# Expert token rows taken from a scattered DRAM buffer and eight transposes instead of sixteen 0/1 matmuls per turn

## The reference

```python
top_logit, top_e = lax.top_k(logits, TOP_K)              # 2 of 8 experts for each token
gate = jax.nn.softmax(top_logit, axis=-1)
...
xb = xt[buf_tok].reshape(n_blk, MOE_BLOCK, d)            # blocks of 128 token rows of one expert
def expert_block(args):
    xblk, e = args
    g, u = jnp.split(xblk @ w_in[e], 2, axis=-1)
    return (jax.nn.silu(g) * u) @ w_out[e]
yb = lax.map(expert_block, (xb, blk_e)).reshape(cap, d)
out = jnp.zeros((n_tok, d), h.dtype).at[buf_tok].add(yb * buf_w[:, None])
```

## Time and profile before

| | us |
|---|---|
| median of 3 runs | 1537.06 (1536.93 to 1539.17) |
| the profiled execution | 1536.48 |
| its span | 1534.8 |
| busy: PE | 1492.7 (97%) |
| busy: DVE | 1202.3 (78%) |
| busy: ACT | 967.4 (63%) |
| busy: POOL | 62.1 (4%) |
| DMA | 425.79 MB, mean 277 GB/s |

### The profile page before, as it was taken

How to read it: one execution, slowest core, us unless ns; L and a number is a source line. 1 busy time by engine, 2 the same in 40 slices (tenths; PEclk the granted TensorE clock), 3 DMA queues, 4 the chain that set the end, 5 groups by cost and what they waited for, 6 DMA issues and landing times.

```text
span 1534.8 us, 20546 instructions
## 1 busy us (share of the span) xinstructions
PE 1492.7 (97%) x7544; PEld 1230.2 (80%) x7544; DVE 1202.3 (78%) x1073; ACT 967.4 (63%) x895; POOL 62.1 (4%) x90
## 2 busy tenths in 40 slices
PE   8999999999999899999999999999999999999995
PEld 6867889998767588888888888888888888888884
DVE  5757464554656799898899888989989989988988
ACT  4645444443344477777677777777777777777774
POOL 1023200000021100000000000000000000000000
PEclk9999999999989999999999999999999999999998
DMA  9741255556503599999999999999999999999990
GB/s 328 176 140 56 70 178 178 180 192 185 172 18 139 207 350 350 341 377 348 362 352 344 377 350 354 343 363 366 342 350 371 345 342 380 344 376 347 335 344 27
DMA packets 200922, 425.79 MB, mean 277 GB/s; under 512 B 10384, under 2 KB 42160, under 8 KB 200880
## 3 DMA queue, kind: packets, MB, share of 16 engines
q1 hardware_dynamic: 196864, 419.65, 76.3%
q10 hardware_dynamic: 4016, 5.56, 1.1%
HBM read 424.14 MB, written 1.05 MB: 277 GB/s over the span
## 4 chain that ended last, share of the span: by engine, by line
PE 90%; DVE 4%; ACT 4%; issue 1%; DMA 1%; ACTq 0%; DVEq 0%
PE bank L922 26%; PE bank L924 26%; PE bank L923 26%; PE bank L1137 2%; PE bank L939 2%; PE bank L1309 2%; ACT wh L863 2%; PE bank L1168 2%; PE bank L1371 2%; DVE wl L1858 1%; PE bank L951 1%; DVE wl L1402 1%; ACT L863 1%; PE bank L1324 0%; PE bank L1325 0%
## 5 line engine op out<-in xcount | busy, mean ns | idle before, releaser
L922 PE MATMUL bank<-wh,arena_r 128*128 128x512 f32 x1432 | 564.4, 394 | 2.6 <-DVE wl L1858 1.4
L1858 DVE TENSOR_TENSOR wl<-ring,wh 128x2048 fp32r<-128x2048 f32 x224 | 511.3, 2291 | 66.3 <-ACT wh L863 65.7
L924 PE MATMUL bank<-wl,arena_r 128*128 128x512 f32 x1432 | 558.1, 390 | 0.0
L923 PE MATMUL bank<-wh,arena_r 128*128 128x512 f32 x1432 | 557.5, 389 | 0.0
L863 ACT ACTIVATE wh<-ring 128x2048 fp32r<-128x2048 f32 x224 | 428.9, 1917 | 92.5 <-PE bank L924 92.4
L922 PEld LDWEIGHTS bank<-wh,arena_r 128*128 128x128 f32 x1432 | 268.9, 188 | 61.5 <-DVE wl L1858 6.4
L924 PEld LDWEIGHTS bank<-wl,arena_r 128*128 128x128 f32 x1432 | 268.8, 188 | 57.0
L923 PEld LDWEIGHTS bank<-wh,arena_r 128*128 128x128 f32 x1432 | 269.1, 188 | 53.7
L1402 DVE TENSOR_TENSOR wl<-ring,wh 128x2048 fp32r<-128x2048 f32 (+1 forms) x64 | 144.5, 2263 | 94.1 <-ACT wh L651 94.0
L651 ACT ACTIVATE wh<-ring 128x2048 fp32r<-128x2048 f32 (+1 forms) x64 | 120.8, 1893 | 114.6 <-PE bank L924 110.0
L1858 DVE TENSOR_TENSOR wl<-arena,wh 128x2048 fp32r<-128x2048 f32 x64 | 146.6, 2291 | 20.2 <-ACT wh L863 20.2
(11 more groups left out here) (246 smaller groups left out, 1363.5 us busy)
## 6 DMA issues: line engine op xcount, KB each, us to landing
ring<-in_moe_w_in_dram SPq DMA_DIRECT2D x171, 1024.0 KB
ring<-in_moe_w_out_dram SPq DMA_DIRECT2D x56, 1024.0 KB
arena<-in_moe_w_out_dram SPq DMA_DIRECT2D x40, 1024.0 KB, 6.0
slot<-in_moe_w_in_dram SPq DMA_DIRECT2D x32, 1024.0 KB, 5.2
arena<-in_moe_w_in_dram SPq DMA_DIRECT2D x24, 1024.0 KB, 6.3
ring<-in_dense_w_in_dram SPq DMA_DIRECT2D x22, 1024.0 KB
slot<-in_moe_w_out_dram SPq DMA_DIRECT2D x16, 1024.0 KB, 5.9
ring<-in_dense_w_out_dram SPq DMA_DIRECT2D x11, 1024.0 KB
```

The lines of the kernel that those rows point to most:

```text
L922: pe.matmul(out_, lh, rh, start=start, stop=False, skip_group_check=True)
L923: pe.matmul(out_, ll, rh, start=False, stop=False, skip_group_check=True)
L924: return pe.matmul(out_, lh, rl, start=False, stop=stop, skip_group_check=True)
L1858: dve.tensor_tensor(wl[:, n % SPLITS, :], slot_at[SLOT[k % PER_EXPERT]], wh[:, n % SPLITS, :].bitcast(F32), ALU.subtract).then_inc(split, 1)
```

## The change

1. A DRAM buffer `xb` of 17 blocks of 128 rows by 1024 float32 (8.9 MB) is filled with zeros: POOL clears 512 columns of the arena (`zeros`) after the first layer norm, and ACT issues two DMAs at c = 3 of the dense mixer, each of 128x17 pieces of 2 KB.
2. DVE works out, ahead of the loop of turns, the row of `xb` for each of the two experts of each token (eight small instructions behind `take_rows(1)`); POOL then issues four indirect DMAs, each of which scatters 128 rows of 4 KB of `h` into `xb`.
3. SP loads 128 rows (512 KB) for the next turn into `xg`, which is `h[:, 0, :]`, ahead of item 16 of each turn. In turn 0 it waits there for the four scatters, for `pre`, and for the first gather.
4. In the loop PE does eight transposes of `xg` (`turn_rows`) instead of `gather`, after a wait for that load. The gather ahead of the loop stays. `build_pick` leaves the loop on DVE.

The diff, cut to its core:

```diff
+ROWS_AT = 16
...
+        zeros = room(12288, 512)
+        xg = h[:, 0, :]
...
+        xb = nc.dram_tensor("xb", [(2 * NE + 1) * P, D], F32)
+        xb_by_turn = xb.rearrange("(s p) n -> s p n", p=P)
...
             for k in range(PER_EXPERT):
+                if k == ROWS_AT:
+                    sp.wait_ge(scattered, 16 * 4)
+                    sp.wait_ge(e_added, 1)
+                    sp.wait_ge(e_rows, 2)
+                    sp.dma_start(xg, xb_by_turn[1]).then_inc(xg_landed, 16)
                 expert_item(0, k, 0, first=True)
...
                 for k in range(PER_EXPERT):
+                    if k == ROWS_AT:
+                        sp.wait_ge(e_rows, 2 * i + 2)
+                        sp.dma_start(xg, xb_by_turn[ds(i + 1, 1)].rearrange("e p n -> (e p) n")).then_inc(xg_landed, 16)
                     expert_item(i, k, i % NE)
...
+            pool.wait_ge(h_ready, 4)
+            pool.memset(zeros, 0.0).then_inc(zeros_ready, 1)
             pool.wait_ge(h_ready, 8)
...
             pool.tensor_scalar(pre[:, :, :], h[:, :, :], ALPHA, None, ALU.mult).then_inc(e_added, 1)
+            pool.wait_ge(zero_filled, 16 * 2)
+            pool.wait_ge(rows_ready, 1)
+            for tt in range(NT):
+                for k in range(2):
+                    pool.indirect_dma_start(xb[:, :], bass.IndirectOffsetOnAxis(ap=rows_i[:, k, tt, :], axis=0),
+                                            h[:, tt, :], None).then_inc(scattered, 16)
...
                     act_e.activation(silu[:, c % 2, :], bank[2 * (c % 2)][:, :], ACT.Silu).then_inc(silu_ready, 1)
+                    if c == 3:
+                        act_e.wait_ge(zeros_ready, 1)
+                        for half in range(2):
+                            act_e.dma_start(xb_by_turn[:, :, 512 * half:512 * half + 512].rearrange("s p n -> p s n"),
+                                            zeros.rearrange("p (s n) -> p s n", s=1).to_broadcast([P, 2 * NE + 1, 512]))\
+                                 .then_inc(zero_filled, 16)
...
+            def turn_rows(i):
+
+                pe.wait_ge(xg_landed, 16 * i + 16)
+                for c in range(DC):
+                    ins = pe.transpose(bank[2 + c // 4][:, (c % 4) * P:(c % 4) * P + P], xg[:, c * P:c * P + P], ident[:, :])
                     if c % 4 == 3:
                         ins.then_inc(e_rows, 1)
...
-                            gather(i + 2)
+                            turn_rows(i)
...
             take_rows(1)
+
+            step(dve.tensor_scalar(best, at_rank, float(P), float(NE * P - P), ALU.is_gt, ALU.mult))
+            step(dve.tensor_tensor(best, best, at_rank, ALU.add))
+            step(dve.tensor_tensor(best, best, first_row[:, :, :], ALU.add))
+            for k, chosen in enumerate((pick1, pick2)):
+                step(dve.tensor_tensor(rest, best, chosen, ALU.mult))
+                step(dve.tensor_reduce(rows_f[:, k, :, :], rest, X, ALU.add))
+            dve.tensor_copy(rows_i[:, :, :, :], rows_f[:, :, :, :]).then_inc(rows_ready, 1)
...
                         elif what == "build":
-                            build_pick(ds(i + 1, 1), i + 1)
                             dve.wait_ge(e_putT, i + 1)
```

More of the change, by code:

```diff
@@ L199, in decoder_kernel @@
         std = sb("std", [P, NT, 2])
-        lg = sb("lg", [P, 7, NT, NE])
+        lg = sb("lg", [P, 8, NT, NE])
         selb = sb("selb", [P, NT, NE], BF16)
@@ L206, in decoder_kernel @@
         turns_i = sb("turns_i", [P, 1], I32)
+        first_row = sb("first_row", [P, NT, NE])
+        rows_f = sb("rows_f", [P, 2, NT, 1])
+        rows_i = sb("rows_i", [P, 2, NT, 1], I32)
         base = [-(-nc.sbuf_base // 64) * 64]
@@ L362, in decoder_kernel @@
         done = sem("done")
+        zeros_ready = sem("zeros_ready")
+        zero_filled = sem("zero_filled")
+        rows_ready = sem("rows_ready")
+        scattered = sem("scattered")
+        xg_landed = sem("xg_landed")
+        xb = nc.dram_tensor("xb", [(2 * NE + 1) * P, D], F32)
+        xb_by_turn = xb.rearrange("(s p) n -> s p n", p=P)
         in_a = w_in_a[0].rearrange("(c p) n -> p c n", p=P)
@@ L581, in _ @@
                            allow_small_or_imprecise_dtypes=True))
+            step(pool.iota(first_row[:, :, :], [[0, NT], [P, NE]], base=-1, channel_multiplier=0,
+                           allow_small_or_imprecise_dtypes=True))
             step(pool.memset(cmp_in[:, :, :, :], 0.0))
@@ L1301, in _, with gather @@
               .then_inc(ranked, 1)
-            def gather(value):
-                pe.wait_ge(e_pick, value)
+            def gather():
+                pe.wait_ge(e_pick, 1)
                 for c in range(DC):
@@ L1310, in gather @@
                                         pick[:, tt, :], start=(tt == 0), stop=(tt == NT - 1))
+                    if c % 4 == 3:
+                        ins.then_inc(e_rows, 1)
+            def turn_rows(i):
+                pe.wait_ge(xg_landed, 16 * i + 16)
+                for c in range(DC):
+                    ins = pe.transpose(bank[2 + c // 4][:, (c % 4) * P:(c % 4) * P + P], xg[:, c * P:c * P + P], ident[:, :])
                     if c % 4 == 3:
@@ L1330, in _ @@
             keep_warm(2, 4)
-            gather(1)
+            gather()
             pe.wait_ge(plan_ready, 1)
@@ L1741, in _, with build_pick @@
             split_weights(N_FIRST + SPLITS)
-            def build_pick(at, value):
-                if value is not None:
-                    dve.wait_ge(e_rows, 2 * value)
+            def build_pick():
                 for tt in range(NT):
-                    ins = dve.tensor_scalar(pick[:, tt, :], slots[:, :], slotx[:, tt, at], None, ALU.is_equal)
+                    ins = dve.tensor_scalar(pick[:, tt, :], slots[:, :], slotx[:, tt, 0:1], None, ALU.is_equal)
                 ins.then_inc(e_pick, 1)
             logits = bank[6][:, 256:256 + NT * NE].rearrange("p (t e) -> p t e", t=NT)
-            best, pick1, rest, pick2, sel, gw, tmp = (lg[:, k, :, :] for k in range(7))
+            best, pick1, rest, pick2, sel, gw, tmp, at_rank = (lg[:, k, :, :] for k in range(8))
             wide = [P, NT, NE]
@@ L1775, in _ @@
             step(dve.tensor_scalar(tmp, bank[7][:, 0:NT * NE].rearrange("p (t e) -> p t e", t=NT), 1.0, None, ALU.add))
[L1776 to L1779, removed]
+            step(dve.tensor_tensor(at_rank, tmp, sel, ALU.mult))
+            step(dve.tensor_scalar(slotx[:, :, 0:NE], at_rank, -1.0, None, ALU.add))
+            build_pick()
+            step(dve.tensor_scalar(slotx[:, :, NE:2 * NE], at_rank, -1.0 - P, None, ALU.add))
             step(dve.tensor_reduce(cnt[:, 0:1], bank[7][:, 2 * NE:3 * NE], X, ALU.max))
```

## The result

The changed kernel takes **1517.45 us** (1515.84 to 1517.85, 4 runs). The kernel before, run beside it, took 1538.12 us (1536.93 to 1539.36, 4 runs). The ratio is 0.9864, 95% interval 0.9846 to 0.9881: 20.7 us faster. The profiled execution took 1517.43 us, its span is 1515.7.

A forecast was written before the change was run, and what follows sets the result against it. PE was taken to bound the kernel, a turn lasting 123.88 us. Only the gather counted: 8 x 2.62 = 21.0 us off 1536.48 gives 1515.5, plus 0.6 for the median, 1516 us; all else nothing; range 1513 to 1528.

The forecast's parts named there:

- Part 1, the gather: End of each turn on PE: 3.50 us of gather become 0.88 of transposes, 2.62 less, 21.0 us in eight turns.
- overshoot: Gain beyond the idle time of ACT and DVE behind the gather, 0.4 to 0.5 us a turn; at most 3.8 us.
- Part 2, the fill: Zero fill issued by ACT in the dense mixer: costs nothing, hidden by ACT's idle time and three split items.
- the low side: Lower bound on ACT's standing at the fill: two issues of 0.45 us, 0.9 us; the upper bound was 16.1.
- The free time: How long ACT may stand at the fill's issues in the dense mixer before PE waits: 9.7 us.
- Part 3, numbers and scatter: Turn 0: eight small instructions in DVE's 4.65 us pause, scatter landing between 533.6 and 555; costs nothing.
- The deadline: Latest end of the scatter in turn 0 that still lets SP load item 16 in time: 558 us.
- Part 4, the row load: SP's extra load in each turn: traffic rises from 355.5 to 367 GB/s, with room; costs nothing.
- DMA as the bound: Rival, in the turns: mixed stream holds only 358 GB/s, a turn takes 124.5 us, 1542 in all; chance 0.09.
- ACT held: Rival, at the fill: ACT's issues hold it until PE stands 6.4 us and the clock falls; 1524; chance 0.14.
- scatter late: Rival, turn 0: at 10 us per indirect DMA the scatter ends 14 us late; 1530; chance 0.06, late fill included.
- Part given back: Rival, at each turn's end: 3.8 us of the gain is lost again, 1520; chance 0.10.

The follow-up runs named there:

- the rest alone: Changed kernel with the gather and its comparisons back in the loop; fill, row numbers, scatter and row loads stay, rows loaded but unused: 1537.31 us, ratio 1.0002.
- the third transfer's run: Changed kernel with one more fill transfer of 4.5 MB, into a second buffer, behind the two on ACT: 1525.99 us, ratio 0.9928.
- sixteen scatters: Changed kernel with twelve more indirect DMAs into other buffers ahead of the four, SP waiting for all: 1521.21 us, ratio 0.9902.
- eight more loads: Changed kernel with eight more SP loads of 512 KB in a turn, which nobody reads: 1516.33 us, ratio 0.9871.
- four more loads: Changed kernel with four more SP loads of 512 KB in each turn (two in the first), which nobody reads: 1516.69 us, ratio 0.9869.
- the cut loop: Changed kernel with ACT's loop of turns cut between items 23 and 24 instead of at the turn's end: 1512.78 us, again 1511.39 us.

## Why the prediction was right

**The forecast case came true, by the mechanism that was forecast.** Predicted 1516.0 against 1537.06 for the kernel before, a gain of 21.0; measured 20.7. The 1.45 us between 1516.0 and 1517.45 are 1.06 of the kernel before's own median (1538.12 this time) and 0.3 to 0.4 of gain.

- *Part 1, the gather.* Forecast 2.62 us a turn, measured 2.59 in the turn's length, and 20.84 / 8 = 2.61 from the first gather to the end. That one part brings the whole gain is shown from both sides: alone it takes 20.7 us off, the rest alone adds 0.2. The overshoot of 0.4 to 0.5 us was booked at nothing because PE has items split ahead. For ACT that was the wrong reason for a right result: the forecast counted one pause of 2.15 us and overlooked the 0.91 us at the second bank. With 3.06 us in all there was no overshoot, and 0.47 us are left. DVE did lose all of its pause, and there the split items must have covered the rest, which no run shows by itself.
- *Part 2, the fill.* Cost nothing, as said, but the step to it was off. I took the low side, 0.9 us of holding, because ACT had once handed over two transfers in 0.45 us or less each. That was the wrong row: those two were 512 KB each, 288 pieces together by the packet records, and the fill's are 2176 pieces each, which held ACT for 4.95 us. The guard that I put beside it (under 6 us even if the second had to wait for part of the first) is what held. The free time was larger than my 9.7 us (my own terms give 261.4 - 1.92 - 2.29 - 0.6 = 256.6, so 10.0): about 12 by the third transfer's run. That the low side itself was wrong did no harm only because of this room.
- *Part 3, numbers and scatter.* The small instructions took 0.17 us each, inside DVE's pause of turn 0, as said. The scatter ended at 543.8, between my bounds of 533.6 and 555. The deadline was 561 rather than 558: the kernel before rounds item 16 at 566.96, not 565.7, and with sixteen scatters that rounding came 4.4 us late and cost PE only 3.8.
- *Part 4, the row load.* 367 GB/s forecast, 367 measured, and no cost at 402 to 404 either.

**The rivals.** DMA as the bound fell twice: the changed kernel's turns ran at 367 GB/s, and eight more loads at 402 to 404 without a change. The figure of the Trainium skill, page "DMA: Bandwidth & Descriptors", section "Specifications", about 358 GB/s for one core, does not bind this kernel; the page's section "Bandwidth" adds that about 358 GB/s is what each core gets where both cores of a pair stream, and only one works here. That clause belonged in my chance for this rival, which was too large at 0.09. The share that I read as 0.96 stands as 0.97 in rows 3; it changes nothing. ACT held, and scatter late, did not happen, but both mechanisms exist and were priced: 21 us of holding cost 8.9 + 1.7 = 10.6 in the profiled execution and 8.8 to 9.6 in the medians of its group, sixteen scatters 4.5 (1521.21 against 1516.69 with four more loads), of which the profile shows 3.8 as PE's wait. "Part given back" fell by the turn's length.

**What the prediction gave no price** was the joint of two turns; its range only allowed "a little gained" there. PE waits there for DVE behind ACT's table load, before the change (6.4 us in all, 14 times) as after it (6.3 us, 14 times), so it took no part in the difference, but the cut loop shows that 3.4 us could be had there. The Trainium skill, page "ScalarE: Activation LUTs", section "What ACT_TABLE_LOAD costs", gives about 1.28 us for the load and 1.38 for a drain. The trace agrees on the 1.28 and shows no drain here: the rounding ahead ends at 650.31, the load runs from 650.32 to 651.60, the next rounding starts at 651.62.

## What to carry to other kernels

When you take work off the engine that bounds the kernel, look at the idle time of the engines that feed it, around the instruction you remove: all of it, as far as they wait for that instruction. If it is as large as the time removed, the gain is the time removed. A DMA issue can hold its engine, here for 0.41 us as the first of three large transfers and for 16.05 us as the third, so price it from a transfer of the same size, not from a small one, and set it against the engine's idle time. A DMA share near 1 is not a limit until a run with more traffic gets slower. And look at the joint of a loop for what each engine pays there once per turn: each engine may cut the same loop where it has slack.

## What the runs showed of the hardware

- **How long an issue holds its engine.** Three transfers of 2176 pieces of 2 KB in a row on ACT held it for 0.41, 4.5 and 16.05 us. By the packet records, 337 pieces of the first transfer had started when the second issue let go at 251.7, so about 1840 were left ahead of it, 115 for each of the 16 DMA engines. The third let go 2.6 us after the first transfer had landed (243.82 + 18.4 = 262.2, against 264.8), again with part of one transfer left ahead of it; by its records (3015 of 4384 started, 16 of those left mark its end) that were some 1350 pieces, 84 for each engine. So the level at which an issue is let go was not the same both times, and why it is that high or low these runs do not show.
- **Two queues shared by pieces, not by bytes.** Between 260 and 275 us of the changed kernel, with the fill (q10, 2 KB pieces) beside SP's loads (q1, 1 KB pieces), the DMA view counts queue, kind, packets, MB and share:

```profile
q10 hardware_dynamic: 1966, 3.99, 68.5%
q1 hardware_dynamic: 1966, 1.98, 37.3%
```

The same number of pieces each, so the fill took two thirds of the bytes. Shorter stretches agree (796 and 795 from 262 to 268 us, 793 and 788 from 268 to 274). SP's loads, issued some 36 us ahead of their use, bore that without a wait of ACT or PE. The Trainium skill, page "DMA: Bandwidth & Descriptors", section "Queues, rings and completion order", has an engine take a whole packet of one queue before it turns to the next; the counts agree with turns of equal numbers of pieces and do not show how many make a packet.
- **Indirect DMA.** 128 rows of 4 KB cost POOL 0.95 to 2.61 us each and 0.30 between two; sixteen in a row took 560.62 + 2.42 - 528.18 = 34.9 us, 2.2 each.
- **The clock.** The same 9 us ran at 0.50 in one execution and at 1.00 in another of the same kernel, and the spans differ by 2.6 us.
